# Three edits to a three-block transformer kernel: the second block's MLP as one program, mixer and compression joined, hgrn's scores added

## The chip, the cores and the metric

The kernel runs on one core of one Trainium2 chip. The metric is the device time of one execution in microseconds, the median of several runs. All data is fp32.

## The reference

Three blocks are applied in turn to x (512 tokens, 1024 features). The parts that the change touches:

```python
# block 1, hgrn mixer: 16 heads of 128, forward (f) and backward (b) gated recurrence over v
intra = einsum('bhts,bhsv->bhtv', where(mask, scores, 0), v)   # per direction, chunkwise
o = o_f + o_b                                                  # both directions
y = (rmsnorm(o, norm_g) * silu(gate)) @ w_out                  # mean square over the head's 128
...
# block 2, gMLP branch: a 128 x 128 lower-triangular token mixing in 4 groups
mixed = einsum('gts,bcsgd->bctgd', tril(ws), v) + bs ;  y_a = gelu(u) * mixed
# block 2, NSA: compression of keys and values, 31 blocks of 32 tokens, per 64-wide head group
k_cmp = gelu((blocks + pe) @ w1) @ w2
...
# block 2, its end
x = x + gt1 * (merged @ w_out)
h = rms_norm(x, g_norm2) * (1 + sc2) + sh2
x = x + gt2 * (square(relu(h @ w_mlp1)) @ w_mlp2)              # 1024 -> 4096 -> 1024
x = rms_norm(x, g_final)
```

## The kernel before, in words

Activations lie transposed: x is `K.xT`, 8 tiles of 128 features by 512 tokens. The work is a row of **phases**. Each is one block of programs, one for each engine, with a barrier at its end; it allocates its own SBUF tiles and all 8 PSUM banks, and takes one of two pools of 32 semaphores (`Kit.phase`, L51). SP clears the other pool (`clear_old`, L60) before its first DMA, so nothing that a phase loads is asked for before the phase begins.

**hgrn_phase** (L439) does 16 heads. PE runs `project(h)` one head ahead of `recur(h-1)`. `project` (L526) makes eight groups of products into banks 0 to 3 (V in 128x128 pieces at L537, the others at L541); a group waits until the bank used four groups earlier has been copied by ACT (`evac`, L531). `recur` (L567) goes through the directions d = 0 and d = 1: transposes (L575, L577), scores into bank SC (L551 to L563), state products (L587, L589), then for both directions four products of v with the masked scores `AT[d]` into OUT (L593) and four of the states S (L598). At its end PE waits for ACT's square of OUT and sums it with one product with ones (L602). DVE masks the scores (L756), copies the first state (L760) and makes the three others one from another (L765), 4 states for each direction; after the mean square and ACT's Ln and Exp (L662, L664) it scales the output (L768, L771) and only then prepares the next head (`prepare`, L706), whose results ACT exponentiates (`exps`, L639) before it copies the next V banks (L626).

**mixer_phase** (L1244): two DMAs, four transposes, then 16 pairs of products (L1271 with 128 rows, L1272 with one row of biases); ACT's gelu, DVE's product. **compress_phase** (L1540): twelve DMAs (L1562 to L1564), two transposes of the positions, then for key and value (n), for each 64-row half (g), 32 products with the tokens (31 columns) and 32 with the position (1 column), all at L1579: 256 products, 512 records. Runs of 64 records lie in the same half of the array. A gelu and two small products follow. Then comes `attention_phase`.

**product_phase** (L786) multiplies one or more matrices of weights with an activation in three fp32r passes (L850, L851, L852: high x high, high x low, low x high), 24 products of 512 columns for an output tile of 128 features ("a unit" below). It first splits the activation into high (ACT, L860) and low (DVE, L896), 8 tiles; weights come in 512 KB pieces (L824), ACT makes the high part (L866), POOL the low part (L834). The programs loop over groups of four units. ACT's high part of a unit waits for the product two units earlier, and the split weights have two buffers. The end of `second_block` (L1857 to L1877) is seven such phases: `wo2` (8 units, with the residual on DVE, L923), `norm_phase` (eight squares on ACT L400, summed on PE L420, Ln L404, Exp L406, scaling L435, shift L411), `m1` (32 units; relu on ACT L1866, square on DVE L1870), four phases `m2` of 8 units, and the last `norm_phase`: 72 units and two norms. The traces call the MLP's tiles m_..., the output product's wo_....

## Time and profile before

| | us |
|---|---|
| median of 3 runs | 4723.94 (4721.99 to 4733.25) |
| the profiled execution, its own time | 4729.1 |
| its span | 4727.4 |
| granted TensorE clock, mean over the span | 0.905 of full |

In the span's numbers, hgrn_phase takes about 254 to 1290 us, mixer and compression 2331 to 2438, attention to 2740, and the stretch from the output product to the last norm of the second block 2838 to 3351. The page gives busy time of each engine; a timeline lists instructions in order of time with the idle time ahead of them and who ended it; a fp32 product appears as two records with a weight load (PEld) each, a fp32r product as one. The clock of a window is 1.00 at 2.4 GHz and 0.50 at 1.2 GHz.

### The profile page before, as it was taken

What the parts mean: (1) busy time and instruction counts of PE and PEld (TensorE: products, weight loads), DVE (VectorE), ACT (ScalarE), POOL (GpSimd) and SP (SyncE); (2) the same over time, 40 slices, a digit from 0 to 9 for tenths busy, and PEclk for the clock granted to TensorE, in tenths of its full rate; (3) what the DMA queues carried; (4) which work ended last, traced back from release to release, by engine and by line L of the source; (5) the groups of instructions that cost most, each with busy time, mean ns of one, the idle gap of its engine ahead of it and who ended that gap; (6) DMA issues with size and microseconds to landing.
All of it is one profiled execution on the core that took longest, in us unless ns stands there. A gap on an engine that the chain in (4) does not pass through costs nothing. (4 is left out here: it accounts for less than half of the span.)

```text
span 4727.4 us, 61028 instructions
## 1 busy us (share of the span) xinstructions
PE 4004.8 (85%) x23891; PEld 2693.9 (57%) x23891; DVE 1669.1 (35%) x3008; ACT 1308.1 (28%) x2192; POOL 603.2 (13%) x326
## 2 busy tenths in 40 slices
PE   6789999999689997778889977988678667877987
PEld 2356666666464443344465555866438447665765
DVE  1024444444516994123213322111227455032222
ACT  0133333333421122222113333222331231324322
POOL 0000000000020000010000022433410110333432
PEclk7799999999899998889869988988889789988998
DMA  8921111111024220112021112322110100222322
GB/s 319 352 62 41 40 44 40 41 44 44 18 58 120 72 71 18 50 36 58 16 55 45 28 53 76 98 76 71 40 29 3 46 10 21 71 71 80 92 72 67
DMA packets 484430, 312.98 MB, mean 66 GB/s; under 512 B 28236, under 2 KB 441477, under 8 KB 484262
## 3 DMA queue, kind: packets, MB, share of 16 engines
q1 hardware_dynamic: 484262, 310.67, 22.3%
q8 instruction: 113, 1.85, 0.2%
q14 instruction: 55, 0.45, 0.0%
HBM read 308.54 MB, written 2.10 MB: 66 GB/s over the span
## 5 line engine op out<-in xcount | busy, mean ns | idle before, releaser
L541 PE MATMUL hg_bank<-hT,hg_w 128*128 128x512 f32 x1024 | 447.3, 592 | 0.0
L998 PE MATMUL cv_bank<-hT,cv_w 128*128 128x512 f32 x768 | 334.0, 596 | 14.1 <-DMA cv_w<-in_conv_w_in_dram 14.1
L541 PEld LDWEIGHTS hg_bank<-hT,hg_w 128*128 128x128 f32 x1024 | 193.3, 190 | 223.6 <-issue 221.9
L1072 DVE SCALAR_TENSOR_TENSOR conv_u<-cv_pad,vec,conv_u 128x512 f32<-128x512 f32 x480 | 318.7, 743 | 0.0
L998 PEld LDWEIGHTS cv_bank<-hT,cv_w 128*128 128x128 f32 x768 | 146.8, 191 | 199.7 <-issue 184.8
L850 PE MATMUL m_bank<-m_rh,m_wh 128*128 128x512 f32 x512 | 205.0, 400 | 63.9 <-POOL m_wl L834 63.9
L851 PE MATMUL m_bank<-m_rl,m_wh 128*128 128x512 f32 x512 | 203.6, 398 | 0.0
L852 PE MATMUL m_bank<-m_rh,m_wl 128*128 128x512 f32 x512 | 203.4, 397 | 0.0
L834 POOL TENSOR_TENSOR m_wl<-m_w,m_wh 128x1024 fp32r<-128x1024 f32 x64 | 152.5, 2386 | 286.3 <-ACT m_wh L866 286.3
L1675 PE MATMUL at_bank<-hT,at_w 128*128 128x512 f32 x384 | 177.1, 605 | 0.0
L834 POOL TENSOR_TENSOR ho_wl<-ho_w,ho_wh 128x2048 fp32r<-128x2048 f32 x8 | 36.6, 4578 | 1079.3 <-ACT ho_wh L866 1079.3
L850 PE MATMUL ff_bank<-ff_rh,ff_wh 128*128 128x512 f32 x352 | 139.1, 395 | 32.8 <-POOL ff_wl L834 32.8
L755 DVE COPY hg_probe<-hg_bank 128x1 f32<-128x1 f32 x32 | 5.1, 158 | 447.0 <-PE hg_bank L556 447.0
L850 PEld LDWEIGHTS m_bank<-m_rh,m_wh 128*128 128x128 f32 x512 | 99.2, 194 | 87.4 <-issue 66.4
L852 PE MATMUL ff_bank<-ff_rh,ff_wl 128*128 128x512 f32 x352 | 137.9, 392 | 0.0
L851 PE MATMUL ff_bank<-ff_rl,ff_wh 128*128 128x512 f32 x352 | 137.9, 392 | 0.0
L537 PE MATMUL hg_bank<-hg_w,hT 128*128 128x128 f32 x1024 | 119.3, 278 | 16.5 <-DMA hg_w<-in_hgrn_w_in_dram 16.5
L537 PEld LDWEIGHTS hg_bank<-hg_w,hT 128*128 128x128 f32 x1024 | 119.1, 195 | 24.1 <-DMA hg_w<-in_hgrn_w_in_dram 16.9
L834 POOL TENSOR_TENSOR ff_wl<-ff_w,ff_wh 128x1024 fp32r<-128x1024 f32 x44 | 104.0, 2384 | 181.9 <-ACT ff_wh L866 181.9
L420 PE MATMUL norm_bank<-norm_sq,ones 128*128 128x512 f32 (+1 forms) x160 | 90.0, 721 | 40.8 <-ACT norm_sq L400 40.5
L1380 PE MATMUL ml_bank<-hT,ml_w 128*128 128x512 f32 x256 | 118.9, 616 | 3.6 <-ACT ml_o L1442 3.0
L314 PE MATMUL ada_bank<-ada_w,ada_cond 128*32 128x512 f32 x480 | 90.5, 893 | 32.2 <-DMA ada_w<-in_w_ada_dram 26.2
(668 smaller groups left out, 8001.3 us busy)
## 6 DMA issues: line engine op xcount, KB each, us to landing
ada_w<-in_w_ada_dram SPq DMA_DIRECT2D x24, 2048.0 KB, 19.6
hg_w<-in_hgrn_w_in_dram SPq DMA_DIRECT2D x80, 512.0 KB, 3.7
m_w<-in_w_mlp_dram SPq DMA_DIRECT2D x64, 512.0 KB, 4.1
ada_w<-in_ada_w_dram SPq DMA_DIRECT2D x12, 2048.0 KB, 19.8
cv_w<-in_conv_w_in_dram SPq DMA_DIRECT2D x48, 512.0 KB, 3.9
ff_w<-in_w_ffn_in_dram SPq DMA_DIRECT2D x44, 512.0 KB, 4.9
at_w<-in_w_in_dram SPq DMA_DIRECT2D x24, 512.0 KB, 3.9
fo_w<-in_w_ffn_out_dram SPq DMA_DIRECT2D x16, 704.0 KB, 4.7
```

Source lines behind the costliest of these rows:

```text
L314: ins = pe.matmul(ps[s][g:g + 32, :], cond[:, k, :], w[s][:, k, :], start=(k < COLS), stop=(k >= KD - COLS))
L420: pe.matmul(ps[j][:, 0:w], K.ones[:, :], sq[:, n % 2, 0:w], start=(k == 0), stop=(k == KD - 1)).then_inc(summed, 1)
L537: ins = pe.matmul(bank[:, t * P:(t + 1) * P], src[:, k, t * P:(t + 1) * P], W[m][:, k, :], start=(k == 0), stop=(k == KD - 1))
L541: ins = pe.matmul(bank[:, 0:w], W[m][:, k, :], src[:, k, 0:w], start=(k == 0), stop=(k == KD - 1))
L834: ins = pool.tensor_tensor(WL[s % 2][g][:, :, :], W[s % raws][g][:, :, :], WH[s % 2][g][:, :, :].bitcast(F32), ALU.subtract)
L850: pe.matmul(ps[p * 4 + g][:, :], WH[p][g][:, k, :], rh[:, k, :], start=(k == 0), stop=False)
L851: pe.matmul(ps[p * 4 + g][:, :], WH[p][g][:, k, :], rl[:, k, :], start=False, stop=False)
L852: ins = pe.matmul(ps[p * 4 + g][:, :], WL[p][g][:, k, :], rh[:, k, :], start=False, stop=(k == kt - 1))
L998: ins = pe.matmul(ps[n % RING][:, :], W[n % SLOTS][:, k * P:(k + 1) * P], K.hT[:, k, :], start=(k == 0), stop=(k == KD - 1))
L1072: ins = dve.scalar_tensor_tensor(o, x, by, o, ALU.mult, ALU.add)
L1380: ins = pe.matmul(SIDE_BANK[n % 2][:, :], W[n % WS][:, k, :], K.hT[:, k, :], start=(k == 0), stop=(k == KD - 1))
L1675: ins = pe.matmul(SIDE_BANK[:, :], W[n % WS][:, k, :], K.hT[:, k, :], start=(k == 0), stop=(k == KD - 1))
```

## The change

Four edits. (1) In hgrn a new tile `ATS` takes the sum of both directions' masked scores: DVE adds `AT[0]` and `AT[1]` after the mask of d = 1, and PE makes the four products with v once, for d = 1. (2) The mean-square product leaves the end of `recur` and is issued inside the next head's `project`, after the second of the four V pieces; for head 14 it stands ahead of the last `recur`. (3) `mixer_phase` and `compress_phase` become `mix_compress_phase`: one phase, all 14 DMAs issued at its start, and the 256 compression products in an order in which the two halves alternate at each step; all sums lie in one bank, HID. (4) The seven phases at the end of `second_block` become `mlp_phase`: one straight program for each engine, 72 units on one ring with four raw, four high and four low weight buffers and six output banks. First-layer parts and second-layer parts alternate, one part ahead; the relu's square is made twice (DVE straight into the high part, ACT in full), DVE subtracts. Squares for both norms are summed inside the stream, two units late. The first two MLP units run side by side as the split slices of h arrive.

```diff
             def _(pe):                                   # hgrn
+                def mean_square(h):
+                    pe.wait_ge(sq_ok, h + 1)
+                    pe.matmul(SC[:, :], K.ones[:, :], osq[:, :], start=True, stop=True).then_inc(ms_ok, 1)
...
+                                if owed is not None and c == 0 and t == 1:
+                                    mean_square(owed)
...
-                        pe.wait_ge(at_ok, 2 * h + (d + 1))
-                        for c in range(NCH):
-                            pe.matmul(OUT[:, c * HC:(c + 1) * HC], vt[p][:, 2 + c, :], AT[d][:, c, :],
+                        if d == 1:
+                            pe.wait_ge(at_ok, 2 * h + 2)
+                            for c in range(NCH):
+                                pe.matmul(OUT[:, c * HC:(c + 1) * HC], vt[p][:, 2 + c, :], ATS[:, c, :],
...
-                    pe.wait_ge(sq_ok, h + 1)
-                    pe.matmul(SC[:, :], K.ones[:, :], osq[:, :], start=True, stop=True).then_inc(ms_ok, 1)
...
+                    project(2 * j, 0, owed=2 * j - 2)
                     recur(2 * j - 1, 1)
+                    project(2 * j + 1, 1, owed=2 * j - 1)
                     recur(2 * j, 0)
+                mean_square(NH - 2)
                 recur(NH - 1, 1)
+                mean_square(NH - 1)
...
+                        if d == 1:                       # DVE, after the mask of d = 1
+                            dve.wait_ge(back_ok, h + 1)
+                            dve.tensor_tensor(ATS[:, :, :], AT[0][:, :, :], AT[1][:, :, :], ALU.add).then_inc(at_ok, 1)
```

```diff
+def mix_compress_phase(K, vn, gu, kvc, kcmp, vcmp):      # PE, after the mixer's products
...
+                pe.wait_ge(cw_in, 16 * 12)
                 for n in range(2):
-                    for g in range(2):
-                        r = slice(DH * g, DH * g + DH)
-                        for bank, of in ((ps[n], lambda l: kvc[r, n, l:l + 16 * (NCMP - 1) + 1:16]), (ps[2 + n], lambda l: peT[r, n, l:l + 1])):
-                            c = NCMP if bank is ps[n] else 1
-                            for l in range(32):
-                                ins = pe.matmul(bank[r, 0:c], w1[n][r, l, :], of(l), start=(l == 0), stop=(l == 31))
+                    for l in range(32):
+                        for r in halves:
+                            pe.matmul(HID[r, NCMP * n:NCMP * (n + 1)], w1[n][r, l, :], kvc[r, n, l:l + 16 * (NCMP - 1) + 1:16],
+                                      start=(n == 0 and l == 0), stop=(l == 31), skip_group_check=True)
+                pe.wait_ge(pos_ok, 1)
+                for n in range(2):
+                    for l in range(32):
+                        for r in halves:
+                            ins = pe.matmul(HID[r, 2 * NCMP + n:2 * NCMP + n + 1], w1[n][r, l, :], peT[r, n, l:l + 1],
+                                            start=False, stop=(l == 31), skip_group_check=True)
```

```diff
+def mlp_phase(K, merged):
+    RAW, SPLIT, BANKS, PARTS = 4, 4, 6, 4
+    order = [(WO, 0), (M1, 0), (M1, 1), (M2, 0), (M1, 2), (M2, 1), (M1, 3), (M2, 2), (M2, 3)]
+    units = [(kind, part, i) for kind, part in order for i in range(KD)]
...
+                for u in range(NU):                      # SP
+                    if u >= RAW:
+                        sp.wait_ge(low, u - RAW + 1)
+                    sp.dma_start(W[u % RAW][:, :, :], weights_of(u)).then_inc(w_in[u % RAW], 16)
...
+                for i in range(KD):                      # PE, output product
+                    ready(i)
+                    for k in range(KD):
+                        if i == 0:
+                            pe.wait_ge(g_low, k + 1)
+                        step(i, k, GH, GL)
+                    if i >= 2:
+                        squares(0, i - 2)
+                squares(0, KD - 2)
+                squares(0, KD - 1)
+                ready(KD)
+                ready(KD + 1)
+                for k in range(KD):
+                    pe.wait_ge(h_low, k + 1)
+                    step(KD, k, HH, HL)
+                    step(KD + 1, k, HH, HL)
+                for u in range(KD + 2, NU):
...
+                    if kind == M2 and part == PARTS - 1 and i >= 2:
+                        squares(1, i - 2)
...
+                for u in range(KD):                      # ACT
+                    weights_high(u + SPLIT - 1)
+                    if u >= 2:
+                        square(0, u - 2)
...
+                for k in range(KD):
+                    modulated(k)
+                weights_high(KD + SPLIT - 1)
+                for u in range(KD + 1, NU):
+                    weights_high(u + SPLIT - 1)
+                    if kind == M1:
+                        hidden(KD * part + i)
...
+                for k in range(KD):                      # DVE, h = scaled + shift, split
+                    if k + 1 < KD:
+                        if k >= 1:
+                            dve.wait_ge(h_low, k)
+                        scaled(k + 1)
+                    modulated_low(k)
...
-        product_phase(K, "wo2", [mat(inp["w_out_2"][0], merged)], KD, on_act, on_dve, "dve")
-    norm_phase(K, [(K.xT, K.hT, T, K.at["g2_2"], M2 + 24, M2 + 32, 2)])
...
-        product_phase(K, "m1", [mat(inp["w_mlp1_2"][0], K.hT)], 32, on_act, on_dve, "act",
-                      extra={"dve": lambda dve, own: dve.sem_inc(own[1], 2)})
...
-        for part in range(4):
-            product_phase(K, "m2", [mat(inp["w_mlp2_2"][0][part * DM:(part + 1) * DM], hid[:, part * KD:(part + 1) * KD, :])],
-                          KD, on_act, on_dve, "dve")
-    norm_phase(K, [(K.xT, K.xT, T, K.at["final_2"], None, None, 2)])
+    mlp_phase(K, merged)
```

## Rows read from the trace of the kernel before

**Rows 1.** The page, part 1: busy time, share of the span, instructions of each engine

```profile
PE 4004.8 (85%) x23891; PEld 2693.9 (57%) x23891; DVE 1669.1 (35%) x3008; ACT 1308.1 (28%) x2192; POOL 603.2 (13%) x326
```

**Rows 2.** The waits of PE from 2830 to 3360 us: total, times, longest

```profile
PE m_bank L850 <- POOL m_wl L834: 63.9, 5, 18.2
PE norm_bank L420 <- ACT norm_sq L400: 15.7, 3, 9.2
PE wo_bank L850 <- POOL wo_wl L834: 15.6, 1, 15.6
```

**Rows 3.** Timeline of PE: start, us, what, [idle before <- releaser]

```profile
2848.24 0.79 PE L850 MATMUL wo_bank<-wo_rh,wo_wh 128*128 128x512 f32 x1 [15.61 <-POOL wo_wl L834]
...
2896.66 10.17 PE L420 MATMUL norm_bank<-norm_sq,ones 128*128 128x512 f32 x16 [3.28 <-ACT norm_sq L400]
```

**Rows 4.** Timeline of DVE and ACT around the two norms of this stretch

```profile
2888.23 0.75 DVE L923 SCALAR_TENSOR_TENSOR xT<-wo_bank,mod,xT 128x512 f32 x1 [4.69 <-PE wo_bank L852]
2893.65 0.75 DVE L923 SCALAR_TENSOR_TENSOR xT<-wo_bank,mod,xT 128x512 f32 x1 [4.68 <-PE wo_bank L852]
...
2906.87 0.69 ACT L404 ACTIVATE norm_root<-norm_bank,epsc 128x512 f32<-128x512 f32 x1 [1.22 <-PE norm_bank L420]
...
3346.05 5.39 DVE L435 SCALAR_TENSOR_TENSOR xT<-xT,norm_gain,norm_rstd 128x512 f32<-128x512 f32 x8 [12.36 <-ACT norm_rstd L406]
```

**Rows 5.** Windows: stretch, length, busy PE, PEld, DVE, ACT, POOL, clock, DMA share, GB/s; DMA issues

```profile
2848.00:2894.00 46.00, 45.14 (x192) 36.94 (x192) 5.60 (x8) 6.37 (x6) 16.81 (x8) 0.97 0.19 53
2925.00:3102.00 177.00, 176.52 (x768) 145.63 (x768) 21.48 (x31) 47.47 (x62) 73.93 (x31) 0.99 0.30 84
...
m_w<-in_w_mlp_dram SPq DMA_DIRECT2D x64, 512.0 KB, 4.1
```

**Rows 6.** Timeline of SP and PE around the compression, and one window of its products

```profile
2377.20 0.58 SPq L1564 DMA_DIRECT2D cp_pe<-in_nsa_pe_v_dram  x1
...
2381.37 0.42 PE L1570 MATMUL cp_bank<-ident,cp_pe 32*128 32x32 f32 x2 [19.95 <-DMA cp_pe<-in_nsa_pe_v_dram]
...
2382.00:2435.60 53.60, 53.49 (x512) 53.48 (x512) 0.05 (x1) 0.00 (x0) 0.00 (x0) 0.50 0.00 1
...
2438.08 0.76 PE L1688 MATMUL at_bank<-nsa_ksw,nsa_q 64*128 64x128 f32 x2 [0.81 <-PEq L1555]
```

**Rows 7.** Alternating 64-row products of the third block: timeline, then a window

```profile
3554.03 1.98 PE L2405 MATMUL rw_bank<-rw_EA,rw_E 64*64 64x64 f32 x32 [9.00 <-DVE rw_E L2282]
3555.79 1.92 PE L2412 MATMUL rw_bank<-stack_ident,rw_a 64*64 64x64 f32 x32
...
3557.70:3560.00 2.30, 2.30 (x86) 2.30 (x84) 2.30 (x5) 1.19 (x2) 0.00 (x0) 1.00 0.00 0
```

**Rows 8.** Timeline of PE in one head's projections

```profile
437.16 7.31 PE L537 MATMUL hg_bank<-hg_w,hT 128*128 128x128 f32 x64
458.20 7.03 PE L541 MATMUL hg_bank<-hT,hg_w 128*128 128x512 f32 x16
```

**Rows 9.** Timeline of the forward recurrence (d = 0), DVE and PE

```profile
488.09 1.11 DVE L765 SCALAR_TENSOR_TENSOR hg_S<-hg_S,hg_dec,hg_bank 128x128 f32<-128x128 f32 x3
...
489.58 0.49 PE L575 MATMUL hg_bank<-ident,hg_ks 128*128 128x128 f32 x3
```

**Rows 10.** Timeline of the backward recurrence (d = 1), DVE and PE

```profile
494.24 0.72 DVE L756 COPY_PREDICATED hg_AT<-hg_mask,hg_bank 128x512 f32<-128x512 uint32 x1
...
495.27 1.06 PE L593 MATMUL hg_bank<-hg_AT,hg_v 128*128 128x128 f32 x8
496.17 1.29 PE L598 MATMUL hg_bank<-hg_cum,hg_S 128*128 128x128 f32 x8
498.15 1.12 PE L602 MATMUL hg_bank<-hg_osq,ones 128*128 128x512 f32 x2 [0.69 <-ACT hg_osq L659]
499.11 1.05 PE L537 MATMUL hg_bank<-hg_w,hT 128*128 128x128 f32 x8
```

**Rows 11.** Timeline of ACT: the copies that free the first banks

```profile
452.16 0.85 ACT L626 ACTIVATE hg_v<-hg_bank 128x512 f32<-128x512 f32 x2
```

More of the change, by code:

```diff
@@ L1551, in compress_phase @@
         h1 = K.sb(st, "cp_h1", [P, 2, NCMP])
-        ps = K.psum_banks(st, "cp")
+        ps = K.psum_banks(st, "gm")
+        HID, POS, SECOND = ps[5], ps[6], (ps[7], ps[0])
         sems, old = K.phase()
-        w_in, tr, pt_ok, first, bias_ok, hid, second, done = sems[:8]
+        (gw_in, cw_in, w_turned, wt_ok, mixed, mix_done, gelu, pos_turned, pos_ok, first, bias_ok, hid, second, done) = sems[:14]
+        halves = [slice(DH * g, DH * g + DH) for g in range(2)]
         with nc.Block() as block:
@@ L1566, in _ @@
             @block.tensor
             def _(pe):
-                pe.wait_ge(w_in, 16 * 12)
+                pe.wait_ge(gw_in, 32)
+                for g in range(4):
+                    ins = pe.transpose(ps[0][:, g * P:(g + 1) * P], ws[:, g, :], K.ident[:, :])
+                ins.then_inc(w_turned, 1)
+                pe.wait_ge(wt_ok, 1)
+                for g in range(4):
+                    for c in range(TT):
+                        o = ps[1 + g][:, c * P:(c + 1) * P]
+                        pe.matmul(o, vn[:, c, g * P:(g + 1) * P], wT[:, g, :], start=True, stop=False)
+                        ins = pe.matmul(o, K.ones[0:1, :], bs[:, g, :], start=False, stop=True)
+                    ins.then_inc(mixed, 1)
@@ L1580, in _ @@
+                pe.wait_ge(pos_ok, 1)
+                for n in range(2):
+                    for l in range(32):
+                        for r in halves:
+                            ins = pe.matmul(HID[r, 2 * NCMP + n:2 * NCMP + n + 1], w1[n][r, l, :], peT[r, n, l:l + 1],
+                                            start=False, stop=(l == 31), skip_group_check=True)
                 ins.then_inc(first, 1)
                 pe.wait_ge(hid, 2)
-                for g in range(2):
-                    r = slice(DH * g, DH * g + DH)
-                    pe.matmul(ps[5][r, 0:NCMP], w2[0][r, :], h1[r, 0, :], start=True, stop=True)
@@ L1585, in _ @@
-                for g in range(2):
-                    r = slice(DH * g, DH * g + DH)
-                    ins = pe.matmul(ps[6 + g][0:NCMP, 0:DH], h1[r, 1, :], w2[1][r, :], start=True, stop=True)
+                for r in halves:
+                    pe.matmul(POS[r, 64:64 + NCMP], w2[0][r, :], h1[r, 0, :], start=True, stop=True)
+                for g, r in enumerate(halves):
+                    ins = pe.matmul(SECOND[g][0:NCMP, 0:DH], h1[r, 1, :], w2[1][r, :], start=True, stop=True)
                 ins.then_inc(second, 1)
@@ L1591, in _ @@
             def _(act):
+                for g in range(4):
+                    act.activation(gu[:, g, :], gu[:, g, :], ACT.Gelu_apprx_tanh).then_inc(gelu, 1)
+                act.wait_ge(bias_ok, 1)
                 for n in range(2):
[L1593 to L1594 removed]
+                    act.activation(h1[:, n, :], HID[:, NCMP * n:NCMP * (n + 1)], ACT.Gelu_apprx_tanh, bias=bias[:, n:n + 1]).then_inc(hid, 1)
             @block.vector
             def _(dve):
[L1598 to L1599 removed]
+                dve.wait_ge(w_turned, 1)
+                dve.tensor_tensor(wT[:, :, :], ps[0][:, :].rearrange("q (g t) -> q g t", t=P),
+                                  K.tri[:, :].unsqueeze(1).broadcast_to((P, 4, P)), ALU.mult).then_inc(wt_ok, 1)
+                for g in range(4):
+                    dve.wait_ge(mixed, g + 1)
+                    dve.wait_ge(gelu, g + 1)
+                    dve.tensor_tensor(gu[:, g, :], gu[:, g, :], ps[1 + g][:, :], ALU.mult).then_inc(mix_done, 1)
+                dve.wait_ge(pos_turned, 1)
+                dve.tensor_copy(peT[:, :, :], POS[:, 0:64].rearrange("q (n l) -> q n l", l=32)).then_inc(pos_ok, 1)
                 dve.wait_ge(first, 1)
[L1601 to L1602 removed]
+                dve.tensor_copy(bias[:, :], HID[:, 2 * NCMP:2 * NCMP + 2]).then_inc(bias_ok, 1)
                 dve.wait_ge(second, 1)
[L1604 to L1606 removed]
+                dve.tensor_copy(kcmp[:, :], POS[:, 64:64 + NCMP]).then_inc(done, 1)
+                for g, r in enumerate(halves):
+                    dve.tensor_copy(vcmp[0:NCMP, r], SECOND[g][0:NCMP, 0:DH]).then_inc(done, 1)
 def attention_phase(K, nq, ksw, nvs, nvg, kcmp, vcmp, nO, gates):
```

257 lines of the change are left out of this document (178 added, 79 removed).

## The prediction

> **What bounds the kernel now.** I read the page first: PE is busy 85% of the span [rows 1], so a gain is either time in which PE waits or PE work that goes away. The mean says nothing of where, so I read each of the three places by itself. (a) From output product to last norm I read PE's waits: five times PE waits for POOL's low weights at the head of an MLP phase, 63.9 us in all, once 15.6 us at the output product, and the norms add 15.7 us, of which one wait lies behind this stretch [rows 2]. Within a phase nothing is waited for: 768 products take 176.52 us, and POOL, ACT and DVE are busy 74, 47 and 21 us beside them [rows 5]. The stretch is bound by PE inside the phases and by phase seams between them. (b) Mixer and compression: the timeline shows PE idle for 19.95 us before the compression's first transposes, until the last of the twelve loads has landed, then 512 records in 53.6 us at clock 0.50 with no wait [rows 6]. (c) hgrn is PE-bound: the only wait within a head is 0.69 us ahead of the mean square [rows 10].
>
> **Edit 4, the MLP as one program.** The clock runs from the first output product at 2848.24 [rows 3] to the first scaling of the last norm at 3346.05 [rows 4]: 497.8 us. The start itself I leave where it is: the first load, ACT's and POOL's first splits are the same chain, and the table load put ahead of them lies in the wait for that load. The new path, term by term:
> - Output product: 192 products 45.14 us [rows 5], and inside it five sums of squares ahead of its last unit. A fp32 product of 512 columns is two records, 16 of them in 7.03 us [rows 8], so 0.86 us each: 4.3. Together 49.4.
> - From the last product to the first slice of h: hand-over and residual 1.0 [rows 4], square 0.7, its sum 1.1, Ln 0.7 [rows 4], Exp 0.7, scaling 0.7 (5.39 for 8 [rows 4]), shift 0.7, low part 0.8; 6.4. Square, Exp and shift are ACT operations of the same 512 columns as the Ln and take its price. Sum 55.8.
> - The first two MLP units: DVE needs a scaling and a low part for a slice, 0.67 + 0.75 and 0.08 for hand-overs, 1.5; PE needs six products, 1.36. DVE sets the pace: 7 x 1.5 + 1.4 = 11.9. Sum 67.7.
> - The other 62 units at (176.52 - 1.8) / 32 = 5.46 us [rows 5]; the 1.8 is what a start at half clock costs, 45.14 less eight times the 5.42 between two residuals [rows 4, 5]. 338.5. Sum 406.2.
> - Five sums of squares within the last eight units 4.3, then residual, square, sum, Ln and Exp 4.2. Sum 414.7.
>
> Saved: 497.8 - 414.7 = 83.1 us. Four MLP seams, each with its cold restart, and two norms are in this. What hides the rest, for each unit of 5.46 us: POOL's low part 2.4 (73.93 / 31), ACT's high part about 1.1 and in a first-layer unit two more of 0.6, DVE at most 1.5, a load that lands 4.1 us after its issue [rows 5] and is asked for four units ahead. ACT's high part of unit u+3 waits for the end of unit u-1 and has three units to spare; behind it in ACT's queue stand only squares and relus that are read a unit later. SP waits for POOL four units back, and nothing else is in its queue. The second-layer parts read hidden tiles that are a whole part old. Straight code in place of loops I cost at nothing: straight programs already issue a record every 0.027 us [rows 7]. If a cover fails it is the first weights after the norm, for which ACT makes units 8 to 10 before the gap. Bounds of this edit: 76 to 90.
>
> **Edit 3, mixer and compression.** PE goes on after the mixer's last product where it was idle for 19.95 us [rows 6]. All of the compression's loading, issue on SP and landing, fitted into that time; now SP issues it behind the mixer's two loads, at about 2334, some 27 us before PE can use it at 2361.4 (2381.37 less the 19.95), so it is there 7 us early; and the mixer's loads stand first in the queue. 20.0 saved, bounds 18 and 20.
>
> The products: 512 records at 53.6 / 512 = 0.105 us, 64 in a row in the same half of the array, clock 0.50 [rows 6]. The third block issues 64x64 products with the halves alternating: 32 records in 1.76 us, 0.055 each, at clock 0.50, and 86 in 2.30 us, 0.027, at 1.00 [rows 7]. No row shows the changed order with 31 or 1 moving columns. Bounds: nothing gained (53.6) and the full clock (13.7). I take 0.055, since the weights loaded have the same 64 columns and the clock in this stretch stayed at 0.50 with PE busy throughout [rows 6]: 28.2 us, so 25.4 saved. One bias copy less is 0.1. Edit 3: 45.4.
>
> Against this order speaks a rule of the Trainium skill, "TensorEngine Tiling (Array Packing)", section "Restrictions and Gotchas": different row tiles cannot access the same PSUM bank simultaneously. HID is one bank for both halves; by that rule alone the 25.4 us would not come. The trace speaks against the rule: the products of rows 7 also write both halves into one bank (L2405), at half the spacing of rows 6.
>
> **Edits 1 and 2, hgrn.** Forward: the four products with v go, eight records of 0.112 us (495.27 to 496.17 [rows 10]), 0.9 us. But the last state product needs DVE's fourth state, which ends at 488.09 + 1.11 = 489.20, and PE's next work starts at 489.58 [rows 9], two records and a hand-over later. The states start when the state product (L589) ends, which doesn't move. PE now idles there instead: saved 0; had the states not been last it would be 0.9 x 16 = 14.
>
> Backward: the mask ends at 494.96; the add takes 0.7 (as the scaling in rows 4), and PE's products with the sum start at 495.75, not 495.27. The first state copy, behind the add on DVE, starts some 0.2 later and so do all four states; PE's sixteen records then set the end: the last starts at 495.75 + 15 x 0.112 = 497.43, before it was 0.28 ahead of 498.15 - 0.69, 497.19 [rows 10]. Cost 0.24 a head.
>
> The mean square: the next projection started at 499.11 [rows 10]; now 0.11 after that last record, 497.54, so 1.57 earlier; the two records of the sum, 0.86, now lie in the projection. Net 0.71 for each of the 14 heads whose sum moves, 9.8 us; heads 14 and 15 pay 0.24 each. Edits 1 and 2: 9.3.
>
> What the delay hides behind: the sum comes at 3.6 us into the projection (32 records) instead of 0.96 before it, so Ln, Exp, DVE's output and the next `prepare`, which stands behind it on DVE, and ACT's copies of V behind that, all come 4.5 us later against the projection. The first V copy ended at about 452.8 [rows 11], and its bank is needed by the fifth group, at 458.20 [rows 8], now 0.9 later: 5.4 - 4.5 + 0.9 = 1.8 us to spare. Cost 0; beyond 1.8 us each us costs 14. SP's loads are not touched.
>
> **Sum.** 83.1 + 45.4 + 9.3 = 137.8 us. The durations are of one execution of 4729.1 us (span 4727.4, the rest lies around it), so 4591.3; it stood 5.2 above the median of 4723.94, within the spread of the three runs, so **4586**.
>
> **Rivals.**
> - The halves don't overlap (the one bank, or one or 31 moving columns): the compression keeps 0.105 a record. For: 0.105 us is what these very products take [rows 6]. Against: rows 7. 4586 + 25 = 4611. Chance 0.10.
> - The compression reaches the full clock, as the alternating products did within 4 us [rows 7]: 512 x 0.027 = 13.7, 14.5 less: 4572. Against: the clock stayed at 0.50 for all 53.6 us before. 0.10.
> - The late mean square stalls the projection: the chain is over 1.8 us longer than I have it. At 1 us over, 14 x 1: 4600. 0.05.
> - Seams stay in the MLP stream at the eight changes of kind, PE waiting some 3 us for split weights or hidden tiles; the change then doesn't do what it says. 4586 + 24 = 4610. 0.02.
> - Slower: the weight ring works as if one deep, because SP, ACT and POOL wait for each other in a circle: a unit then takes landing 4.1 + high 1.1 + low 2.4 + hand-overs 0.2 = 7.8 us, 2.3 more for 72 units, 168 us: 4754. It decides from 137.8 / 72 = 1.9 us a unit, spacing 7.4. Against: four buffers at each stage and POOL idle for 103 of the first layer's 177 us [rows 5]. 0.03.
>
> My forecast has the rest, 0.70. The range, 4562 to 4618: below, the full clock (14.5) and the upper bound of edit 4 (7); above, no overlap (25) and the lower bound of edit 4 (7). A measurement of this kernel can tell about 0.3%, 14 us, from no change. Every case but the ring's lies over 100 us below the kernel before: faster 0.96, same 0.01, slower 0.03.
>
> **What would show it.** PE's waits between output product and last norm: one of about 16 at the start, one of 4 to 7 between output product and MLP, none at part borders; clock 1.00 from there on, units 5.4 to 5.5 apart. Compression: transposes right behind the mixer, 512 records in 28 us; 54 means no overlap, 14 the full clock. hgrn: projections of successive heads 61.25 us apart instead of 61.95 (437.16 [rows 8] and 499.11 [rows 10]), products with v at d = 1 half a us after the state products, a new PE idle of 0.5 at d = 0, none before the mean square. Wrong is the forecast if MLP units are over 6 us apart, if heads are not closer together, or if the compression keeps its spacing.

## The result, and the profile after

| | before | after |
|---|---|---|
| median | 4725.81 (4721.99 to 4733.25, 4 runs) | 4594.64 (4588.50 to 4596.94, 4 runs) |
| the profiled execution, its own time | 4729.1 | 4588.5 |
| its span | 4727.4 | 4586.9 |
| mean granted clock | 0.905 | 0.916 |

The ratio is 0.9719, 95% interval 0.9702 to 0.9735: 131.2 us less by the medians. The prediction was 4586, 137.8 us less, range 4562 to 4618.

The two traces can be cut at the same events in both. The numbers below are my own sums, each the difference of two start times (the first product of a tile's bank, or the last write of a tile), in us:

| stretch | before | after | difference | predicted |
|---|---|---|---|---|
| hgrn, first product to last output | 1021.18 | 1014.01 | -7.2 | -9.3 |
| from there to the mixer's first product, untouched | 1049.39 | 1042.33 | -7.1 | 0 |
| mixer's first product to attention's first | 101.77 | 55.02 | -46.8 | -45.4 |
| attention, untouched | 410.17 | 410.00 | -0.2 | 0 |
| first output product to the next block's first split | 529.24 | 447.85 | -81.4 | -83.1 |
| from there to the end, untouched | 1349.92 | 1352.33 | +2.4 | 0 |

Ahead of the first row lie 265.74 and 265.34 us, so the two spans differ by 140.5 us. The three edited stretches give 135.3 us, within 2.5 of the sum. The last edited row ends behind the last norm's scaling; up to that scaling, where the prediction ended its sum, it is 497.81 before and 416.28 after. An untouched stretch moved by as much as the whole hgrn edit; the last section takes it up.

The page after, part 1; it answers to [rows 1]:

```profile
PE 3951.6 (86%) x23763; PEld 2643.7 (58%) x23763; DVE 1740.9 (38%) x3022; ACT 1303.9 (28%) x2183; POOL 604.5 (13%) x326
```

PE's busy time fell by 53.2 us, DVE's rose by 71.8 with only 14 instructions more. Half of the first is the compression's; most of the second has a cause of its own, shown with e8.

**The MLP.** PE's waits from before the output product to the next block's first norm, columns as in [rows 2]:

```profile
PE mp_bank L1879 <- POOL mp_wl L1863: 14.9, 1, 14.9
PE norm_bank L420 <- ACT norm_sq L400: 9.1, 1, 9.1
PE mp_bank L1879 <- DVE mp_hl L1995: 3.9, 1, 3.9
```

The five waits at phase heads, 63.9 us, are gone. The first line is the start that I left alone (15.6 before), the second belongs to the next block's norm, the third is the one wait between output product and MLP. The timeline, columns as in [rows 3], with DVE's last scaling:

```profile
2786.70 0.80 PE L1879 MATMUL mp_bank<-mp_dh,mp_wh 128*128 128x512 f32 x1 [14.89 <-POOL mp_wl L1863]
...
2837.68 2.93 PE L1887 MATMUL mp_bank<-mp_sq,ones 128*128 128x512 f32 x6
2844.54 0.76 PE L1879 MATMUL mp_bank<-mp_hh,mp_wh 128*128 128x512 f32 x1 [3.93 <-DVE mp_hl L1995]
...
3202.98 5.39 DVE L2030 SCALAR_TENSOR_TENSOR xT<-xT,vec,mp_rstd 128x512 f32<-128x512 f32 x8 [3.40 <-ACT mp_rstd L1940]
```

From 2786.70 to 3202.98 are 416.28 us. Windows over the whole of this stretch, first before, then after, columns as in [rows 5], say what the difference to 497.81 consists of:

```profile
2848.24:3346.05 497.81, 425.80 (x1760) 340.17 (x1760) 82.48 (x123) 131.81 (x172) 169.09 (x71) 0.91 0.26 72
2786.70:3202.98 416.28, 410.93 (x1760) 333.21 (x1760) 144.19 (x121) 126.90 (x162) 170.58 (x71) 0.99 0.30 87
```

The same 1760 records stand in both. PE is idle for 72.0 us before and for 5.4 after: 66.6 of the 81.5 us. The other 14.9 are shorter busy time at a clock of 0.99 instead of 0.91; before, it read 0.50 for 13.7 us at each of the four seams between MLP phases.

In the timeline above, the second and third line show the last six of the sixteen records that sum the squares, and the MLP starting after a wait of 3.93 us behind them. Windows of a part of the MLP and of the compression, columns as in [rows 5]:

```profile
2860.00:3145.00 285.00, 285.00 (x1259) 236.06 (x1258) 117.28 (x86) 89.28 (x114) 127.65 (x53) 1.00 0.34 99
2347.00:2374.00 27.00, 27.00 (x509) 27.00 (x510) 0.65 (x2) 0.00 (x0) 0.00 (x0) 0.50 0.01 2
```

In 285 us of the MLP PE is never idle and the clock is 1.00; beside it DVE is busy 117 us.

**The compression**, timeline of PE, answering to [rows 6]:

```profile
2346.00 0.79 PE L1546 MATMUL gm_bank<-gm_bias,ones 1*128 1x128 f32 x2
2346.59 0.36 PE L1550 MATMUL gm_bank<-ident,cp_pe 32*128 32x32 f32 x2
2346.88 13.86 PE L1555 MATMUL gm_bank<-nsa_kvc,cp_w 64*64 64x31 f32 x256
2360.55 13.80 PE L1561 MATMUL gm_bank<-cp_peT,cp_w 64*64 64x1 f32 x256
...
2376.70 0.76 PE L1678 MATMUL at_bank<-nsa_ksw,nsa_q 64*128 64x128 f32 x2 [0.81 <-PEq L1523]
```

The transposes follow the mixer's last record at once. 256 records take 2360.55 - 2346.88 = 13.67 us, 0.053 each, where they took 0.105. The clock in the window above stayed at 0.50 with PE busy for all of it.

**hgrn**, timeline of PE, then of DVE, for the head of [rows 9] and [rows 10]:

```profile
486.52 1.64 PE L606 MATMUL hg_bank<-hg_cum,hg_S 128*128 128x128 f32 x8 [0.38 <-DVE hg_S L771]
...
494.15 1.16 PE L601 MATMUL hg_bank<-hg_ATsum,hg_v 128*128 128x128 f32 x8 [0.30 <-DVE hg_ATsum L768]
495.15 1.06 PE L606 MATMUL hg_bank<-hg_cum,hg_S 128*128 128x128 f32 x8
496.11 3.83 PE L542 MATMUL hg_bank<-hg_w,hT 128*128 128x128 f32 x32
499.78 1.02 PE L529 MATMUL hg_bank<-hg_osq,ones 128*128 128x512 f32 x2
...
493.41 0.69 DVE L768 TENSOR_TENSOR hg_ATsum<-hg_AT 128x512 f32<-128x512 f32 x1
494.02 0.28 DVE L771 COPY hg_S<-hg_bank 128x128 f32<-128x128 f32 x1
```

PE's waits over all heads:

```profile
PE hg_bank L606 <- DVE hg_S L771: 6.1, 16, 0.4
PE hg_bank L601 <- DVE hg_ATsum L768: 4.9, 16, 0.3
PE hg_bank L529 <- ACT hg_osq L667: 1.4, 2, 0.7
```

Before, PE waited 11.0 us for the square. Now it waits 6.1 for the last state at d = 0 and 4.9 for the sum of the scores, 0.4 and 0.3 a head; the square is waited for only by the last two heads.

### The profile page after: what moved, and what is told of

The parts are those of the page before. It is cut to its first block and busy times, and to the rows that moved or that the text cites. A ratio compares the mean times of both kernels' runs of the same rounds, so it can differ in the third digit from the quotient of the medians.

```text
span 4586.9 us, 59667 instructions
## 1 busy us (share of the span) xinstructions
PE 3951.6 (86%) x23763; PEld 2643.7 (58%) x23763; DVE 1740.9 (38%) x3022; ACT 1303.9 (28%) x2183; POOL 604.5 (13%) x326
## 5 line engine op out<-in xcount | busy, mean ns | idle before, releaser
L1863 POOL TENSOR_TENSOR mp_wl<-mp_w,mp_wh 128x1024 fp32r<-128x1024 f32 x72 | 173.0, 2405 | 242.4 <-ACT mp_wh L1928 242.4
L1928 ACT ACTIVATE mp_wh<-mp_w 128x1024 fp32r<-128x1024 f32 x72 | 76.3, 1060 | 252.9 <-PE mp_bank L1881 250.5
L1879 PE MATMUL mp_bank<-mp_dh,mp_wh 128*128 128x512 f32 x320 | 129.9, 406 | 14.9 <-POOL mp_wl L1863 14.9
L1880 PE MATMUL mp_bank<-mp_dl,mp_wh 128*128 128x512 f32 x320 | 125.7, 393 | 0.0
L1881 PE MATMUL mp_bank<-mp_dh,mp_wl 128*128 128x512 f32 x320 | 125.7, 393 | 0.0
L845 POOL TENSOR_TENSOR qk_wl<-qk_w,qk_wh 128x1024 fp32r<-128x1024 f32 x8 | 18.9, 2360 | 743.1 <-ACT qk_wh L877 743.1
```

What stands on the lines that cost most here:

```text
L845: ins = pool.tensor_tensor(WL[s % 2][g][:, :, :], W[s % raws][g][:, :, :], WH[s % 2][g][:, :, :].bitcast(F32), ALU.subtract)
L1863: pool.tensor_tensor(WL[u % SPLIT][:, :, :], W[u % RAW][:, :, :], WH[u % SPLIT][:, :, :].bitcast(F32), ALU.subtract).then_inc(low, 1)
L1879: pe.matmul(bank[:, :], wh[:, k, :], rh[:, k, :], start=(k == 0), stop=False)
L1880: pe.matmul(bank[:, :], wh[:, k, :], rl[:, k, :], start=False, stop=False)
```

## The experiments

Each is made from the changed kernel. "Stretch" is a row of the table above. A single run is read by its trace; only the three with an interval are compared in whole time.

**e5, the MLP program alone.** hgrn, mixer and compression are those of before.

```diff
-    mix_compress_phase(K, vn, gu, kvc, kcmp, vcmp)
+    mixer_phase(K, vn, gu)
+    compress_phase(K, kvc, kcmp, vcmp)
...
     (hgrn_phase as before)
```

> The kernel before with only edit 4, the program for output product, norms and MLP. Theory: the edits are independent. From the first output product to the next block's first product preparation 448 us as in the change (529 before), the hgrn heads 61.95 us apart, 102 us from the mixer's first product to the attention's; the time 81 us below the kernel before (ratio 0.983). Rival: part of the gain hangs on what stands ahead (clock, loads): then this stretch differs from 448 us by more than 2.

Measured: 4651.59 (4645.13 to 4654.96), ratio 0.984, interval 0.9824 to 0.9856. The stretch is 446.28 us against 529.24: 83.0 us, as against 81.4 with all edits in. hgrn (1021.03) and mixer to attention (101.57) are those of before. It lies 1.7 us from the 448 expected, so the rival (over 2) fell: this edit's gain does not depend on the other edits. By the two ratios these bring another 0.984 - 0.9719 = 1.21%, 57 us, where 54.7 were predicted.

**e6, sums of squares after the stream.** The squares of both norms are summed at the end of their part, not inside it.

```diff
                     step(i, k, GH, GL)
-                    if i >= 2:
-                        squares(0, i - 2)
-                squares(0, KD - 2)
-                squares(0, KD - 1)
+                for i in range(KD):
+                    squares(0, i)
...
     (the same for the second norm, and for ACT's squares)
```

> The change with the sums of squares of both norms taken out of the stream of products: all eight follow the last unit, as in the norm phases, but in the same program. Theory: a sum costs PE 0.86 us wherever it stands, so the stretch stays within 0 to 2 us of the change's 448; what was saved was the phases' seams. Rival: the sums in the stream were hidden in some gap of PE, and putting them late costs their length, about 5 x 0.86 twice = 8.6 us.

Measured: 4599.21, one run; the stretch is 449.27 us against 447.85. Most of these 1.4 us are the clock: with unchanged MLP code the stretch lay between 446.28 (e5) and 449.20 us (e1), by when the clock rose. The last sum starts 416.01 us after the first output product; in e1, whose clock rose at nearly the same places, 415.82. So the place of the sums is worth about 0.2 us, not the 8.6 of the rival: a norm's sixteen records cost PE the same wherever they stand, and PE never waits for a square. The gain of this edit is the seams.

**e7, the first two MLP units one after another.**

```diff
-                    step(KD, k, HH, HL)
-                    step(KD + 1, k, HH, HL)
+                for u in (KD, KD + 1):
+                    ready(u)
+                    for k in range(KD):
+                        if u == KD:
+                            pe.wait_ge(h_low, k + 1)
+                        step(u, k, HH, HL)
```

> The change with the first two MLP units one after another instead of side by side. Theory: DVE hands out a slice of h every 1.45 us; one unit alone uses 0.68 of it, so the first takes 11.6 to 12 us and the second 5.44 more, 17.2 for both instead of 11.9: the stretch 5.2 us longer. Rival: PE is the bound in these units (it starts at half clock): no more than 1 us.

Measured: 4593.35, one run. The waits for slices of h, from the timeline of PE:

```profile
2843.90 0.77 PE L1879 MATMUL mp_bank<-mp_hh,mp_wh 128*128 128x512 f32 x1 [3.94 <-DVE mp_hl L1995]
2849.61 0.50 PE L1879 MATMUL mp_bank<-mp_hh,mp_wh 128*128 128x512 f32 x1 [0.18 <-DVE mp_hl L1995]
...
2852.51 0.50 PE L1879 MATMUL mp_bank<-mp_hh,mp_wh 128*128 128x512 f32 x1 [0.48 <-DVE mp_hl L1995]
```

Once at full speed the single unit waits up to 0.48 us a slice for DVE. The third MLP unit starts 15.74 us after the first; side by side it was 12.3 in the changed kernel, and 12.6 to 13.9 in the nine others, by when the clock rose. Side by side is worth 1.8 to 3.4 us; against e2, where the first MLP product starts at the same 56.7 us, it is 2.4. Both numbers expected were wrong, the 5.2 us and the rival's 1. The units alone took less than the 17.2 I had: six slices at DVE's pace, 8.61 us, the last slice 0.88 behind (DVE has no further scaling to do ahead of it), 0.81 for its products and 5.44 for the second unit, 15.74. And side by side took more than the 11.9.

**e8, low weights on DVE.** POOL does nothing in this stretch.

```diff
-                for u in range(NU):                      # gpsimd
-                    pool.wait_ge(high, u + 1)
-                    pool.tensor_tensor(WL[u % SPLIT][:, :, :], W[u % RAW][:, :, :], ..., ALU.subtract).then_inc(low, 1)
+                def weights_low(u):                      # vector
+                    dve.wait_ge(high, u + 1)
+                    dve.tensor_tensor(WL[u % SPLIT][:, :, :], W[u % RAW][:, :, :], ..., ALU.subtract).then_inc(low, 1)
```

> The change with the low parts of the weights made by DVE instead of POOL, POOL idle in the stretch. In the change's trace DVE's square of the relu takes 2.51 us in 30 of 32 cases, always with POOL's 2.40 us subtraction begun 0.44 us ahead, and 0.68 us in the two cases without it. Theory: DVE's two-operand SBUF instruction stands still until POOL's is done; without POOL all 32 take 0.68 us, and since PE bounds the stream the stretch changes by no more than 2 us (about 1 less at the start, where DVE's subtraction is shorter than POOL's). Rival: the instruction is slow by itself (same operand twice, rounded output): 2.51 us stays.

What it was made for stands in the changed kernel: the groups of POOL and DVE in the stretch (busy us, mean ns, idle before), and below them a piece of the timeline.

```profile
L1863 POOL TENSOR_TENSOR mp_wl<-mp_w,mp_wh 128x1024 fp32r<-128x1024 f32 x72 | 173.0, 2405 | 242.4 <-ACT mp_wh L1928 242.4
L2001 DVE TENSOR_TENSOR mp_dh<-mp_relu 128x512 fp32r<-128x512 f32 x32 | 76.7, 2398 | 74.1 <-ACT mp_relu L1950 74.1
```

```profile
2874.56 2.40 POOL L1863 TENSOR_TENSOR mp_wl<-mp_w,mp_wh 128x1024 fp32r<-128x1024 f32 x1 [3.04 <-ACT mp_wh L1928]
2875.00 2.51 DVE L2001 TENSOR_TENSOR mp_dh<-mp_relu 128x512 fp32r<-128x512 f32 x1 [2.13 <-ACT mp_relu L1950]
2877.62 0.69 DVE L2004 TENSOR_TENSOR mp_dl<-mp_relu,mp_dh 128x512 fp32r<-128x512 f32 x1
```

DVE's square of 128x512 takes 2.51 us, begins while POOL's subtraction is under way and ends 0.55 us after it; 30 of the 32 do (median 2.512, shortest 0.678). Of the two short ones, one meets no POOL work and one begins 0.44 us before POOL's subtraction. In e8 the groups are:

```profile
L1980 DVE TENSOR_TENSOR mp_wl<-mp_w,mp_wh 128x1024 fp32r<-128x1024 f32 x72 | 88.2, 1225 | 190.3 <-ACT mp_wh L1921 190.2
L2003 DVE TENSOR_TENSOR mp_dl<-mp_relu,mp_dh 128x512 fp32r<-128x512 f32 x32 | 22.2, 692 | 3.3
L2000 DVE TENSOR_TENSOR mp_dh<-mp_relu 128x512 fp32r<-128x512 f32 x32 | 21.9, 684 | 0.0
```

Measured: 4600.46, one run. With POOL idle the same square takes 0.68 us and the low weights 1.23 instead of 2.40, and the two parts of DVE's square together 44 us instead of 103, yet the stretch is 447.30 against 447.85: what DVE loses to POOL is real and hidden, 3.2 us (2.51 + 0.69) in a unit of 5.44. No row shows it as a wait; it stands in the durations. The Trainium skill's page "SBUF — State Buffer", section "SBUF: two separate sides", says that the port pair shared by VectorE and GpSimd is an exclusive lock, taken also by a VectorE operation with two SBUF inputs against a GpSimd operation that reads SBUF. The trace agrees: 2.51 us for the square behind POOL, 0.68 with POOL idle.

**e3, products in runs.** Alternation undone, the joined phase kept.

```diff
                 for n in range(2):
-                    for l in range(32):
-                        for r in halves:
+                    for r in halves:
+                        for l in range(32):
...
     (the same for the 256 products of the positions)
```

> The joined phase with the compression's products in runs of 64 records in the same half of the array, as before; the same bank, the same count. Theory: the alternation is what halves the spacing, so the 512 records take 53.6 us again instead of 27.5, and the span is 26 us longer than the change's; the idle 20 us ahead of the transposes stay away. Rival: it was the one bank, or the order of token and position products, that made them quicker: then 27.5 us stays.

Timeline of PE:

```profile
2351.34 25.99 PE L1555 MATMUL gm_bank<-nsa_kvc,cp_w 64*64 64x31 f32 x253
...
2377.39 24.75 PE L1561 MATMUL gm_bank<-cp_peT,cp_w 64*64 64x1 f32 x242
```

Measured: 4613.3, one run. The first 256 records take 26.05 us, 0.102 each, and the second as long (the window behind the second line ended before they did). Mixer to attention is 79.52 against 55.02. The 24.5 us belong to the order of the halves alone; nearly all of the 0.105 of [rows 6] is the price of runs in one half. By subtraction, 101.77 - 79.52 = 22.2 us are left; 20.15 are the join, and the other 2.1, in which positions are copied beside products and banks change less often, were not taken apart.

**e4, a bank for each half.**

```diff
-                        for r in halves:
+                        for HID, r in zip(HIDS, halves):         # HIDS = (ps[5], ps[7])
                             pe.matmul(HID[r, NCMP * n:NCMP * (n + 1)], ...
...
     (gelu and bias copy split in two, one for each half)
```

> The change with the sums of the two halves in two different banks instead of one. Theory: the bank plays no part, 512 records again in 27.3 to 27.7 us; about 0.5 us more behind them, since gelu and bias copy become two instructions each. Rival (halves that share a bank hold each other up): the records get quicker, towards 14 us.

Timeline of PE:

```profile
2354.74 13.86 PE L1555 MATMUL gm_bank<-nsa_kvc,cp_w 64*64 64x31 f32 x256
2368.41 13.79 PE L1561 MATMUL gm_bank<-cp_peT,cp_w 64*64 64x1 f32 x256
2383.89 0.32 PE L1566 MATMUL gm_bank<-cp_h,cp_w 64*64 64x31 f32 x2 [1.68 <-ACT cp_h L1578]
```

Measured: 4600.53, one run. 13.67 us for 256 records, to the hundredth what one bank takes. The stretch is 0.93 us longer, for the gelu and the copy in two parts. Whether the halves share a bank plays no part in this pace. Why alternation halves the spacing, no run shows.

**e9, the mixer's products grouped by shape.** For each bank, the four products of 128 rows, then the four of one row.

```diff
                     for c in range(TT):
-                        o = ps[1 + g][:, c * P:(c + 1) * P]
-                        pe.matmul(o, vn[:, c, g * P:(g + 1) * P], wT[:, g, :], start=True, stop=False)
-                        ins = pe.matmul(o, K.ones[0:1, :], bs[:, g, :], start=False, stop=True)
+                        pe.matmul(ps[1 + g][:, c * P:(c + 1) * P], vn[:, c, g * P:(g + 1) * P], wT[:, g, :],
+                                  start=(c == 0), stop=False, skip_group_check=True)
+                    for c in range(TT):
+                        ins = pe.matmul(ps[1 + g][:, c * P:(c + 1) * P], K.ones[0:1, :], bs[:, g, :],
+                                        start=False, stop=True, skip_group_check=True)
```

> The change with the mixer's products in another order: for each bank first the four with 128 rows, then the four with one row (the biases); the same 32 products. In the change each record there takes 0.36 us at clock 0.50, where 128 columns of weights and 128 of data at that clock would be 0.21. Theory: going from 128 rows to one row and back costs about 0.3 us each time; with 8 changes instead of 32 the mixer's 64 records take some 15 us instead of 23.1, and the span is 8 us shorter. Rival: the one-row products are slow by themselves: 23 us stays.

```profile
2329.17 2.08 PE L1544 MATMUL gm_bank<-gm_wT,gm_v 128*128 128x128 f32 x8 [0.78 <-DVE gm_wT L1585]
2331.17 2.07 PE L1547 MATMUL gm_bank<-gm_bias,ones 1*128 1x128 f32 x8
...
2345.06 0.36 PE L1552 MATMUL gm_bank<-ident,cp_pe 32*128 32x32 f32 x2
```

Measured: 4587.89, one run. Eight records take 2.00 us, 0.25 each; in the changed kernel's order they took 0.36. Mixer to transposes is 17.80 us against 24.91. So going back and forth between products of 128 rows and of one row costs, 7.1 us for 32 products; by the 24 changes saved, 0.30 each. This edit also parts two products that add to the same place of a bank. That this is not the cause is argued from [rows 8], where records that add to one place eight products long come 0.11 us apart at clock 1.00; no run tests it alone.

**e1, scores not added.** Eight records with v for each direction, as before; the mean square stays delayed.

```diff
-                        if d == 1:
-                            pe.wait_ge(at_ok, 2 * h + 2)
+                        pe.wait_ge(at_ok, 2 * h + (d + 1))
...
-                                pe.matmul(OUT[:, c * HC:(c + 1) * HC], vt[p][:, 2 + c, :], ATS[:, c, :],
-                                          start=False, stop=False, skip_group_check=True)
+                                pe.matmul(OUT[:, c * HC:(c + 1) * HC], vt[p][:, 2 + c, :], AT[d][:, c, :],
+                                          start=(d == 0 and c == 0), stop=False, skip_group_check=True)
...
-                            dve.tensor_tensor(ATS[:, :, :], AT[0][:, :, :], AT[1][:, :, :], ALU.add).then_inc(at_ok, 1)
```

> The change without its edit 1: no sum of the two directions' scores, four products of v in each direction again; the mean square stays delayed. Theory: the add costs time, because at d = 0 the removed products only make room for a wait on the fourth state, while at d = 1 PE waits for the add (0.30 us idle, the first products 0.48 us later than before). Without it the stretch from the state product to the next projection at d = 1 goes from 3.6 us (1.68 + 1.00 + 0.93) to 3.24 (1.22 + 0.89 + 1.13, the last bound by DVE's states), heads from 61.42 us apart on the mean to about 61.05, and hgrn takes 16 x 0.37 = 6 us less than in the changed kernel; d = 0 stays at 3.24 us. Rival: the eight fewer records of PE are worth their own length: then this kernel is slower than the change by up to 16 x 0.9 = 14 us, heads 62.3 apart.

Timeline of PE at the end of d = 1:

```profile
494.82 1.06 PE L599 MATMUL hg_bank<-hg_AT,hg_v 128*128 128x128 f32 x8
495.71 1.29 PE L604 MATMUL hg_bank<-hg_cum,hg_S 128*128 128x128 f32 x8
497.22 3.83 PE L541 MATMUL hg_bank<-hg_w,hT 128*128 128x128 f32 x32 [0.21 <-issue]
```

Measured: 4591.96 (4589.81 to 4594.21), ratio 0.9711, interval 0.9694 to 0.9727; not to be told from the change's 0.9719. The trace tells them apart: hgrn takes 1010.55 us, 3.5 less than with the sum, where 6 were expected; the rival, up to 14 us slower, fell. The products with v start right behind the state products (494.82). The new 0.21 us ahead of the next projection I put down to the loop's own step: PE's program loops over two heads, and the spacing alternates 61.00 and 61.34 to 61.38, longer each time the loop turns. Before, all heads stand 61.95 to 61.96 apart, so it must have lain inside the 0.69 us wait for the square.

**e2, mean square at the end of its head, sum kept.**

```diff
-                    project(2 * j, 0, owed=2 * j - 2)
+                    project(2 * j, 0)
...
                     ins.then_inc(out_ok, 1)                  # end of recur
+                    mean_square(h)
```

> The change without its edit 2: the mean square stands at the end of each head's recurrence again, the scores are still added. Theory: the delay is worth PE's idle time and the hand-over around the square, 0.95 us a head, and the add costs 0.35; heads then stand 61.95 + 0.4 = 62.3 us apart, hgrn is 12 to 13 us longer than in the change. Rival: the add pays for itself once PE has no other wait: then heads stand at or below 61.95.

```profile
498.61 1.16 PE L601 MATMUL hg_bank<-hg_ATsum,hg_v 128*128 128x128 f32 x8 [0.31 <-DVE hg_ATsum L767]
...
501.35 1.12 PE L529 MATMUL hg_bank<-hg_osq,ones 128*128 128x512 f32 x2 [0.69 <-ACT hg_osq L666]
502.31 2.95 PE L542 MATMUL hg_bank<-hg_w,hT 128*128 128x128 f32 x25
```

Measured: 4604.57, one run. Heads are 62.30 us apart, against 61.96 before and 61.42 in the change; hgrn takes 1025.97 us, 12.0 more than in the change. The 0.69 us wait is back. So the delay is worth 0.89 a head with the sum in place, and the sum costs 0.34 a head without the delay; with it, 61.42 - 61.19 = 0.23 (e1). In edits 1 and 2 the second pays for the first.

**e10, all that helped.** e1 and e9 together, and the compression's position term by DVE: it multiplies the weights by the position and sums over the 32 steps, and PE adds the result with 8 records in place of 256.

```diff
+                for n in range(2):                       # vector
+                    dve.tensor_tensor(prod[:, n, :, :], w1[n][:, :, :], peT[:, n, :].unsqueeze(2).broadcast_to((P, 32, DH)), ALU.mult)...
+                for n in range(2):
+                    dve.tensor_reduce(wpe[:, n, :], prod[:, n, :, :].rearrange("q l j -> q j l"), AX.X, ALU.add)...
...
-                            ins = pe.matmul(HID[r, 2 * NCMP + n:2 * NCMP + n + 1], w1[n][r, l, :], peT[r, n, l:l + 1],
+                        ins = pe.matmul(HID[r, 2 * NCMP + n:2 * NCMP + n + 1], wpe[r, n, :], K.ones[r, 0:1],
```

> A version meant to beat both: the change without the added scores (6 us), with the mixer's products grouped (8 us), and with the 128 position products of the compression (256 records, 13.8 us) replaced by DVE: w1 times the position, summed over the 32 steps, 4 DVE instructions of about 2.2 us each beside the token products, then 4 products with ones. 6 + 8 + 13 = 27 us below the change, ratio to the kernel before about 0.966. Rival: DVE's four instructions outlast the token products' 13.7 us and PE waits: 20 us below the change at most.

Timeline of PE, then of DVE:

```profile
2342.84 13.86 PE L1554 MATMUL gm_bank<-nsa_kvc,cp_w 64*64 64x31 f32 x256
2356.51 0.57 PE L1559 MATMUL gm_bank<-ones,cp_wpe 64*64 64x1 f32 x8
...
2359.43 0.76 PE L1683 MATMUL at_bank<-nsa_ksw,nsa_q 64*128 64x128 f32 x2 [0.81 <-PEq L1520]
...
2343.64 4.49 DVE L1591 TENSOR_TENSOR cp_prod<-cp_w,cp_peT 128x2048 f32<-128x2048 f32 x2
2348.05 7.31 DVE L1595 TENSOR_REDUCE cp_wpe<-cp_prod 128x64 f32<-128x2048 f32 x2
```

Measured: 4573.47 (4567.31 to 4577.76, 5 runs) against 4726.18, ratio 0.9669, interval 0.9656 to 0.9683, apart from the change's 0.9702 to 0.9735. DVE's 11.8 us lie beside PE's 13.7 of the other products. Mixer to attention is 34.68 us, 20.3 less than in the change, and hgrn 4.5 less: 24.8 in these two stretches, 21 in the medians. Of the 27 expected, mixer and compression gave theirs (7.1 and 13.2 for 8 and 13), hgrn 4.5 for 6. The rival, PE waiting for DVE, fell. It is faster than both kernels.

## Why the prediction held, and where its terms were off

The direction, the mechanism of each edit and the sum held; 4594.6 lies 8.6 above the forecast, inside the range. Of the 8.6, 2.5 are the edits' own (137.8 against 135.3). The median before rose by 1.9 with a fourth run, the other way. What remains lies in how untouched stretches fell in these runs, and is about what a measurement can't tell. That the sum came within 2.5 is in part luck: edit 3 gave 1.4 more than forecast, edit 4 1.6 less and hgrn 2.1 less. Two numbers of the forecast don't follow from its own terms: 14 x 0.71 is 9.9 and not 9.8, and the lower bound, 14.5 and 7 below 4586, would be 4564.5 and not 4562. Neither decides anything here.

**Edit 4, predicted 83.1, measured 81.5 to the same event.** Term by term from the first output product (measured values are start times from the changed kernel's trace):

| | predicted | measured |
|---|---|---|
| last output product, five sums ahead of it | 49.4 | 50.7 |
| first MLP product | 55.8 | 57.8 |
| third MLP unit | 67.7 | 70.1 |
| last MLP product, with five sums inside | 410.5 | 411.7 |
| first scaling of the last norm | 414.7 | 416.3 |

The first 1.3 us are TensorE's clock: here products went from 0.43 to 0.23 us apart 6.1 us after the start (the 2793 mark), in the kernel before and in e5 after about 3, and e5 has the whole 83.0. The hand-over through the norm took 0.7 more than I had. The two units side by side took 12.3 instead of 11.9, and gave part of it back later: units are 5.44 us apart, predicted 5.46. The wait behind the norm, foretold at 4 to 7 us, was 3.93. No load, high or low part was ever late: the covers named held, with one mis-sized. **"DVE at most 1.5"** was 3.2 in each first-layer unit, because DVE's square takes 2.51 us beside POOL (e8). It cost nothing only because 2.2 us of the unit were left.

**Edit 3, predicted 45.4, measured 46.8.** The join gave 20.15 (mixer to transposes 45.06 to 24.91; predicted 20.0). A record takes 0.053 us, where I took 0.055 from another block's products [rows 7]. Before, 128 records and not 64 stood in a row in one half, those with the tokens and those with the position of the same half; e3 has runs of 64 and nearly the same pace. e3 shows that the order of the halves is the cause, and e4 that the bank is not, so the rival by which the halves don't overlap fell. The rule of the Trainium skill's page "TensorEngine Tiling (Array Packing)", section "Restrictions and Gotchas", by which different row tiles can't use one bank at the same time, did not cost anything here: 13.67 us for 256 records with one bank and with two. The rival of the full clock fell too: 0.50 over the 27 us.

**Edits 1 and 2, predicted 9.3, measured 7.2.** The step at d = 0 held: PE idles 0.38 us before the states' products, and from the first state product to the end of these it takes 3.24 us as before. At d = 1 the sum's price of 0.24 a head was 0.34 (e2: 62.30 - 61.96): eight records from 494.15 to 495.15 take 1.00 us instead of 0.90, the first behind a wait. The mean square's delay was to give 0.95 before that price (0.71 + 0.24); it gave 0.77 in e1, since the loop's step came out from under the wait that was removed.

**The term that failed was "now 0.11 after that last record", 497.54 - 495.75 = 1.79 us from the first product with the sum to the next projection.** It left out two things. The first record of the sum, behind its wait, takes 0.22 us and not 0.11 (494.15 to 494.37), in every head. And each time the loop turns, every second head, the next projection comes 0.19 after the last record (0.11 in the other heads), and its first 32 records take 3.67 us (496.11 to 499.78) and not 3.58 (557.53 to 561.11). That is 0.11 a head and on average another 0.09; with small differences of 0.03 the other way heads are 61.42 apart, not 61.25. In e1, where PE has no wait for the sum, the loop's share is larger, 0.18 a head. The rival of the late mean square fell: PE's waits in hgrn hold no bank freed late.

**The ring and seam rivals** fell with the waits: one at the start, one behind the norm, none at the eight changes of kind.

## What to carry to other kernels

Where an engine is bound by products inside phases and waits only at their heads, join the phases and count the seams; placing small sums cleverly inside the stream brought 0.2 us. Small products want an order by the rows they use: alternate halves (0.053 instead of 0.105 us a record) and group equal row counts (0.25 instead of 0.36). Both pairs are at clock 0.50. When a wait is removed, list what else was hidden in it, down to the loop's own step, and test each half of a pair of edits by itself: adding the scores saved PE work that was waiting anyway and cost 3.5 us.

## What the runs showed that I had not expected

**DVE behind POOL**: 0.68 us became 2.51 in 30 of 32 squares, and it shows only as a mean that is too long for the shape (2398 ns for the group).

**An untouched phase with two lengths.** Of the 7.1 us gained between hgrn and mixer, 5.6 lie in one product phase (tile qk_bank, 192 products) and 1.7 in the phase behind it. To the next phase's first product the first is 63.4 us long in the changed kernel and 69.1 in the kernel before. The whole stretch was 1042 to 1043 in four traces, each with this phase at 63.3 to 63.5, and 1047 to 1052 in the other eight, with 67.7 to 70.2. Windows of that phase, first of the changed kernel, then of e8, in which this phase is the same code:

```profile
2080.00:2138.50 58.50, 48.27 (x192) 37.58 (x192) 22.22 (x28) 15.62 (x22) 16.35 (x7) 0.95 0.15 40
```

```profile
2082.00:2147.00 65.00, 56.10 (x192) 43.95 (x192) 23.51 (x28) 15.23 (x21) 16.39 (x7) 0.80 0.13 34
```

The same 192 products are busy 48.3 us at a mean clock of 0.95 in one and 56.1 at 0.80 in the other. In e8 PE waits three times, 2.9 to 3.0 us each, for weights after every second unit, and the clock reads 0.50 for 6.8 us at each of these waits. In the changed kernel it reads 0.50 at the first of them, for 3.4 us; at the second, as long, it stays at 1.00, and PE then waits 1.3 to 1.4 us after each unit. From 20 us into the phase to the end of its products the clock is 1.00. What decides between the two courses was not settled: kernels with the same code before this phase (the change and e4) fell on either side. A difference of 7 us between two single traces of this kernel is thus no effect of an edit until the stretches have been compared.
